# Down projections of the second block by Strassen's scheme over eight pairs of input rows, and gain sums taken as a row that is turned into columns

## The reference

```python
D_FF = 2816
def swiglu(x, w_gu, w_down):
    g, u = jnp.split(x @ w_gu, 2, axis=-1)
    return (jax.nn.silu(g) * u) @ w_down

def second_block(x, ...):
    for l in range(DEPTH):                      # DEPTH = 2
        x = layer_norm(ALPHA * x + 0.5 * swiglu(x, ffn1_w_gu[l], ffn1_w_down[l]), ln1_g[l], ln1_b[l])
        x = layer_norm(ALPHA * x + hybrid_mixer(x, ...), ln2_g[l], ln2_b[l])
        x = layer_norm(ALPHA * x + 0.5 * swiglu(x, ffn2_w_gu[l], ffn2_w_down[l]), ln3_g[l], ln3_b[l])
    return x
```

## Time and profile before

| | us |
|---|---|
| median of 3 runs | 3413.47 |
| lowest, highest | 3411.47, 3414.45 |
| the profiled execution | 3413.02 |
| its span, first to last instruction | 3411.2 |
| PE busy in the span | 3383.5 |
| DVE busy | 2519.0 |
| ACT busy | 1600.6 |
| POOL busy | 433.6 |

### The profile page before, as it was taken

How to read it: one execution, slowest core, us unless ns; L and a number is a source line. 1 busy time by engine, 2 the same in 40 slices (tenths; PEclk the granted TensorE clock), 3 DMA queues, 4 the chain that set the end, 5 groups by cost and what they waited for, 6 DMA issues and landing times.

```text
span 3411.2 us, 50605 instructions
## 1 busy us (share of the span) xinstructions
PE 3383.5 (99%) x19622; PEld 2917.4 (86%) x19622; DVE 2519.0 (74%) x3115; ACT 1600.6 (47%) x2183; POOL 433.6 (13%) x305
## 2 busy tenths in 40 slices
PE   9999999999999999999999999999999999999998
PEld 6888889988788888998899876899889988679986
DVE  8999568934999657963797388898288937978954
ACT  5555444423565444542444256544254524664433
POOL 3333010001333210001000120200020003120002
PEclk9999999999999999999999999999999999999999
DMA  3112334333221233332443221333333232123332
GB/s 127 62 62 68 108 120 161 100 117 117 69 68 62 88 127 124 131 123 98 146 147 118 93 81 56 123 117 100 119 124 112 100 123 89 60 85 138 100 123 99
DMA packets 98845, 357.23 MB, mean 105 GB/s; under 512 B 10960, under 2 KB 14544, under 8 KB 96976
## 3 DMA queue, kind: packets, MB, share of 16 engines
q1 hardware_dynamic: 85824, 305.68, 26.7%
q10 hardware_dynamic: 12816, 48.70, 3.8%
HBM read 321.83 MB, written 16.78 MB: 99 GB/s over the span
## 4 chain that ended last, share of the span: by engine, by line
PE 87%; issue 4%; DVE 3%; POOL 2%; ACT 1%; POOLq 1%; DMA 1%; DVEq 0%; SPq 0%; ACTq 0%
PE ps L2496 15%; PE ps L2498 14%; PE ps L2497 14%; PE ps L2557 10%; PE ps L2558 10%; PE ps L2556 10%; PE sc L2496 3%; PE sc L2497 3%; PE sc L2498 3%; POOLq L1452 1%; PE ps L2735 1%; DVE w_lo L1510 1%; PE sc L2810 1%; POOL DE L1454 1%; POOL Y L1447 1%
## 5 line engine op out<-in xcount | busy, mean ns | idle before, releaser
L1510 DVE TENSOR_TENSOR w_lo<-raw,w_hi 128x1024 fp32r<-128x1024 f32 x369 | 476.9, 1292 | 472.0 <-ACT w_hi L757 448.2
L757 ACT ACTIVATE w_hi<-raw 128x1024 fp32r<-128x1024 f32 x369 | 390.1, 1058 | 805.8 <-PE sc L2498 402.8
L2496 PE MATMUL ps<-h_hi,w_hi 128*128 128x512 f32 x1352 | 566.3, 419 | 10.9 <-DVE w_lo L1510 5.9
L2498 PE MATMUL ps<-h_hi,w_lo 128*128 128x512 f32 x1352 | 529.3, 391 | 0.0
L2497 PE MATMUL ps<-h_lo,w_hi 128*128 128x512 f32 x1352 | 528.5, 391 | 0.0
L870 ACT ACTIVATE w_hi<-raw 128x1024 fp32r<-128x1024 f32 x204 | 216.4, 1061 | 386.6 <-PE ps L2558 209.2
L2557 PE MATMUL ps<-h_lo,w_hi 128*128 128x256 f32 x1272 | 359.9, 283 | 0.0
L2556 PE MATMUL ps<-h_hi,w_hi 128*128 128x256 f32 x1272 | 359.7, 283 | 0.0
L2558 PE MATMUL ps<-h_hi,w_lo 128*128 128x256 f32 x1272 | 359.7, 283 | 0.0
L2496 PEld LDWEIGHTS ps<-h_hi,w_hi 128*128 128x128 f32 x1352 | 254.7, 188 | 84.7 <-issue 29.9
L2497 PE MATMUL ps<-hid_lo,w_hi 128*128 (+1 forms) x792 | 308.2, 389 | 0.0
(11 more groups left out here) (393 smaller groups left out, 7647.9 us busy)
## 6 DMA issues: line engine op xcount, KB each, us to landing
raw<-wts SPq DMA_DIRECT2D x471, 512.0 KB, 3.3
S<-wts SPq DMA_DIRECT2D x51, 512.0 KB, 3.3
A<-wts SPq DMA_DIRECT2D x51, 512.0 KB, 3.3
x<-parked ACTq DMA_DIRECT2D x7, 2048.0 KB, 8.7
h_hi<-early_hi ACTq DMA_DIRECT2D x15, 512.0 KB, 3.9
h_lo<-early_lo ACTq DMA_DIRECT2D x15, 512.0 KB, 3.5
parked<-x ACTq DMA_DIRECT2D x24, 256.0 KB, 2.0
parked<-x ACTq DMA_DIRECT2D x3, 2048.0 KB, 8.7
```

What stands on the lines that cost most here:

```text
L757: act(w_hi[:, s].rearrange("p a b -> p (a b)"), raw[:, s, :], ACT.Copy).then_inc(s_whi, 1)
L1510: tt(w_lo[:, s].rearrange("p a b -> p (a b)"), raw[:, s, :], w_hi[:, s].rearrange("p a b -> p (a b)").bitcast(F32), ALU.subtract).then_inc ...
L2496: mm(out, w_hi[:, s, b, :], hi, start=start, stop=False, skip_group_check=True)
L2498: return mm(out, w_lo[:, s, b, :], hi, start=False, stop=stop, skip_group_check=True)
```

## The change

**Down by quads.** For the four feed-forwards of the second block, `down` is replaced by `down_by_quads` on PE, with `down_quads_hi` on ACT, `down_quads_lo` on DVE and `load_down_quads` on SP. The first 6 input tiles are done as before (144 matmuls of 128x512). The other 16 are eight pairs. For six of the eight output tiles, two at a time, three quads of seven products are done over all eight pairs: 21 products of 24 matmuls of 128x256, 504 in all. The last two output tiles take 96 matmuls of 128x512.

The products need sums of the hidden layer: T2, N3 and N4, each 128x2048 (eight pairs x 256 tokens), built from hi and lo parts in ten DVE operations (`token_sum`) and then split again (ACT hi, DVE lo). One difference is put into the hidden layer itself (`token_difference`, 128x256, once for each of eight quads of gate and up). Weight blocks need four sums in each quad. DVE adds each product to x in ten half-width steps a quad (`take`), and the eight plain banks before that with `take_plain`.

**Gain rows.** `gain_sums` is replaced by `gain_rows_of`: gain and bias are the loaded operand (4 or 2 columns) and the weights the moving one (256 columns), 16 matmuls that leave a row in PSUM. ACT copies it (`gain_rows`), and `gain_columns` turns it with two matmuls of 128x2. In the norm, ACT's `h_hi` steps and DVE's `x_lo` steps stand one and two places later.

```diff
+DOWN_QUAD_FFS = (2, 3, 4, 5)
+N_DOWN_QUADS = 3
+DOWN_PLAIN = 6
+DOWN_PAIRS = (FT - DOWN_PLAIN) // 2
+DOWN_TOKEN_SUMS = 10
+DOWN_TAKES = 10
...
+        def down_w(b):
+
+            slot = (0, 2, 1)[b % 3]
+            return (w_hi[:, slot], w_lo[:, slot]) if slot < 2 else (wd_hi[:], wd_lo[:])
...
+                token_hi(TD_hi[:], TD[:], 5)
+                split_hi(pair0 + 1, 1)
+                split_hi(pair0 + 2, 0)
+                token_hi(ND_hi[:], ND[:], 7)
+                split_hi(pair0 + 2, 1)
+                eng.wait_ge(s_used, c0 + 1)
+                a11_hi(0)
+                s2_hi(0)
+                eng.wait_ge(e_used, down_tile(f, KT - 1))
+                s1_hi(0)
+                token_hi(FD_hi[:], FD[:], 9)
+                eng.drain()
+                eng.sem_inc(s_whi, 4 * N_DOWN_QUADS)
+                for q in range(N_DOWN_QUADS):
+                    b = PRODUCTS * q
+                    last = q == N_DOWN_QUADS - 1
...
+                def token_difference(q):
+                    if token_differences(f, q + 1) > token_differences(f, q):
+                        eng.wait_ge(e_ev, ev_done(f, q, TIMES1))
+                        tt(gates[:, 0, HALF:], gates[:, 0, HALF:], gates[:, 0, 0:HALF], ALU.subtract).then_inc(e_ev, 1)
 
...
+
+                for k0 in (0, 4):
+                    first_sums(0, k0)
+                for k0 in (0, 4):
+                    first_sums(1, k0)
+                split_lo(pair0 + 1, 0)
+                for k0 in (0, 4):
+                    first_sums(2, k0)
+                token_sum(ND[:], down_rows_of(hid_hi, 0, 0).bitcast(F32), TD[:], ALU.subtract, 5)
+                split_lo(pair0 + 1, 1)
+                token_lo(0, TD_lo, TD, TD_hi)
+                token_sum(ND[:], ND[:], down_rows_of(hid_lo, 0, 0).bitcast(F32), ALU.add, 6)
+                split_lo(pair0 + 2, 0)
+                eng.wait_ge(e_lo, down_token(f, 0))
+                token_sum(FD[:], down_rows_of(hid_hi, 1, 0).bitcast(F32), TD[:], ALU.subtract, 6)
+                token_lo(1, ND_lo, ND, ND_hi)
+                split_lo(pair0 + 2, 1)
+                token_sum(FD[:], FD[:], down_rows_of(hid_lo, 1, 0).bitcast(F32), ALU.add, 8)
+                s3(0)
+                s1(0)
+                block_lo(0, raw[:, 0, :])
+                eng.wait_ge(s_park, back(f))
+                take_plain(0)
+                s2(0)
+                take_plain(1)
+                block_lo(1, raw[:, 0, :])
+                for j in range(2, 5):
+                    take_plain(j)
+                block_lo(2, SD1[:])
+                for j in range(5, KT):
+                    take_plain(j)
+                token_lo(2, FD_lo, FD, FD_hi)
+                eng.drain()
+                eng.sem_inc(s_wlo, 4 * N_DOWN_QUADS)
+                for q in range(N_DOWN_QUADS):
+                    b = PRODUCTS * q
+                    last = q == N_DOWN_QUADS - 1
+
+                    if q:
+                        take_p6(q - 1)
+                        block_lo(b + 2, SD1[:])
+                        eng.wait_ge(e_ev, taken(q - 1, 9))
+                        if q == 1:
+                            eng.sem_inc(s_xp, 2)
+                        else:
+                            eng.sem_inc(s_xp, 1)
+                    block_lo(b + 3, SD3[:])
+                    take_p0(q)
...
+                        centre(0)
+
+                    take_p1(q)
+                    block_lo(b + 4, raw[:, 1, :])
...
+                c0 = pair0 * 2
+                eng.wait_ge(s_pair, FT * (f + 1) + 1)
+                eng.wait_ge(s_hidl, f * FT + DOWN_PLAIN)
+                for i in range(DOWN_PLAIN):
+                    s = i % 2
+                    eng.wait_ge(s_wlo, c0 + i + 3)
+                    for n in DOWN_ORDER:
+                        if i == 0 and n == 0:
+                            eng.wait_ge(e_act, act_done(f, quads(f) - 1, SILU0))
+                            eng.wait_ge(e_ev, ev_done(f, quads(f) - 1, TAKE_C12))
+                        if i == 0 and n == 2:
+                            eng.wait_ge(s_pair, FT * (f + 1) + 2)
+                        last = three(ps[n][:], s, n, hid_hi[:, i, :], hid_lo[:, i, :], i == 0, i == DOWN_PLAIN - 1)
+                        if i == DOWN_PLAIN - 1:
+                            last.then_inc(e_used, 1)
+                    if i < DOWN_PLAIN - 1:
+                        last.then_inc(s_used, 1)
+                eng.wait_ge(s_hidl, FT * (f + 1))
+
...
+                def product(b, bank, hi, lo, fresh):
+                    wh, wl = down_w(b)
+                    eng.wait_ge(e_lo, down_block(f, b))
+                    out = ps[bank][:, 0:HALF]
+                    for k in range(DOWN_PAIRS):
+                        mm(out, wh[:, k, :], hi[:, k, :], start=fresh and k == 0, stop=False, skip_group_check=True)
+                        mm(out, wh[:, k, :], lo[:, k, :], start=False, stop=False, skip_group_check=True)
+                        last = mm(out, wl[:, k, :], hi[:, k, :], start=False, stop=k == DOWN_PAIRS - 1, skip_group_check=True)
+                    last.then_inc(e_used, 1)
+
...
+                for q in range(N_DOWN_QUADS):
+                    b = PRODUCTS * q
+                    X, Y, Z = DOWN_BANKS[q]
+                    eng.wait_ge(e_ev, (down_taken(f, 3), down_taken(f, 6), down_take(f, 0, DOWN_TAKES - 1))[q])
+                    product(b, Y, *hid(0, 0), True)
+                    eng.wait_ge(e_lo, down_token(f, 0))
+                    product(b + 1, X, TD_hi, TD_lo, True)
+                    product(b + 2, Z, *hid(0, 1), True)
+                    eng.wait_ge(e_lo, down_token(f, 1))
+                    eng.wait_ge(e_ev, down_take(f, q, 3))
+                    product(b + 3, X, ND_hi, ND_lo, False)
+                    product(b + 4, Y, *hid(1, 0), False)
+                    eng.wait_ge(e_lo, down_token(f, 2))
+                    eng.wait_ge(e_ev, down_take(f, q, 6))
+                    product(b + 5, X, FD_hi, FD_lo, False)
...
+            def gain_rows_of(i, L, c):
+
+                eng.wait_ge(s_gl, DEPTH)
+                for k in range(KT):
+                    mm(ps[6][0:4, 0:2 * P], gb[:, L, i, k:k + 25:8], w_hi[:, :, k, :], start=(k == 0), stop=False,
+                       skip_group_check=True)
+                    last = mm(ps[6][0:2, 0:2 * P], gb[:, L, i, k:k + 9:8], w_lo[:, :, k, :], start=False,
+                              stop=(k == KT - 1), skip_group_check=True)
+                last.then_inc(s_used, 1)
+
+            def gain_columns(n):
+
+                eng.wait_ge(s_fgc, n + 1)
+                for s in range(2):
+                    last = mm(ps[6][:, 2 * P + 2 * s:2 * P + 2 * s + 2], gain_rows[:, s * P:(s + 1) * P], picks,
+                              start=(s == 0), stop=(s == 1), skip_group_check=True)
+                last.then_inc(s_fst, 1)
...
+
+                eng.wait_ge(s_wlo, c + 3)
                 bank_free()
                 for q in range(KT):
-                    gain_sums(i, L, c, 0, q, q + 1)
                     step(0, q, CENTRED[q])
                     if q == 0:
                         sums(n, order[-1])
+                eng.wait_ge(s_wlo, c + 4)
                 for q in range(KT):
-                    gain_sums(i, L, c, 1, q, q + 1)
                     step(1, q, q)
+                    if q == 1:
+                        gain_rows_of(i, L, c)
+                    elif q == 5:
+                        gain_columns(n)
 
...
+        blocks = [first[half, DOWN_ORDER[2 * q + tile]] for q in range(N_DOWN_QUADS)
+                  for half, tile in ((0, 0), (1, 0), (1, 1), (0, 1))]
+        blocks += [first[half, DOWN_ORDER[j]] for half in range(2) for j in (6, 7)]
+        return [gu.reshape(N_GU, P, CHUNK, P), rows[:DOWN_PLAIN], np.stack(blocks)]
     last = rows[DOWN_ROWS:].transpose(2, 1, 0, 3)[list(DOWN_ORDER)]
     return [gu.reshape(N_GU, P, CHUNK, P), rows[:DOWN_ROWS], last]
```

More of the change, by code:

```diff
@@ L353, in build @@
         folded_sums = small[:, 24:28]
-        low_sums = small[:, 28:32]
+        picks = small[0:4, 28:30]
+        gain_rows = place("gain_rows", [4, 2 * P], at=t_at(17))
         ps = [ctx.enter_context(nc.psum_tensor(f"ps{i}", [P, SEQ], F32)) for i in range(3)]
@@ L1274, in layer_norm @@
                 act(ps[4][:], lnt[:], ACT.Exp, scale=-0.5).then_inc(s_rstd, 1)
-                for j in range(KT + 1):
+                for j in range(KT + 2):
                     if j < KT:
@@ L2217, in layer_norm @@
+            def layer_norm(i, L, c0, order, evacuate, hv, folded_to=(), f=None):
                 n = 3 * L + i
@@ L2280, in layer_norm @@
                 eng.wait_ge(s_rstd, 6 + n)
-                for j in range(KT + 2):
+                for j in range(KT + 4):
                     if j < KT:
@@ L2649, in down, with down_by_quads, hid @@
                     last.then_inc(s_used, 1)
+            def down_by_quads(pair0, f, centre):
+                c0 = pair0 * 2
```

(22 more changed lines are left out.)

389 lines of the change are left out of this document (334 added, 55 removed).

## The result

The changed kernel takes 3430.3 us (median of five runs, 3428.9 to 3431.8), the kernel before 3413.5. The ratio is 1.005, with a 95% interval from 1.0039 to 1.0061: slower by 17 us. The forecast was 3424 in a range from 3408 to 3436, slower being the likeliest, so the time lies 6 us above it and inside the range. The profiled execution took 3430.9 us, its span 3429.1, 17.9 more than that of before.

A forecast was written before the change was run, and what follows sets the result against it. PE's matmul stream was taken to bound the kernel, with no slack for waits. From the profiled 3413.0 us: - 19.6 (down matmuls) - 7 (gain sums) + 32 (waits for DVE) + 6 (clock) = 3424 us, range 3408 to 3436.

The forecast's parts named there:

- Part 1: PE matmuls of the second block's four down projections: 4.9 us gained in each, 19.6 us in all.
- Part 3: DVE's ordered work before each down stage's first product: PE stands still 8.0 us, four times, 32 us lost.
- The cover behind it: Within a down quad, DVE's 15.9 us of work fits beside PE's 20.1 us, so no wait.
- Part 4: PE's clock halves after the gap before the first product: 6 us lost over four stages, bounds 0 and 3 each.
- Part 2: Gain sums done as rows in five norm pairs: 1.4 us gained each, 7 us in all (4.5 to 8.5).
- the turn at 0.5: The two 128x2 matmuls that turn the gain row into columns: taken at 0.5 us, between 0.24 and about 1.0.
- the rest of the norm's tail I cost at nothing: Chunk splits and `h_lo` steps behind the gain sums: same work in another order, no cost.
- PE also waits in the last quad and behind it: Rival: more waits of 1 to 2 us a stage there, 3430; chance 0.12 shared with the columns rival.
- The cover holds: Rival: DVE's work is done beside the plain down matmuls, all or mostly; 3386, up to 3406; chance 0.08.
- No drop of the clock: Rival: as forecast, but PE's clock stays up behind the down stages' gap; 3418; chance 0.14.
- Waits of about 5 to 6 us a stage: Rival: PE waits only this long in each down stage, clock or not; 3407 to 3413, no change; chance 0.08.
- The turn into columns: Rival: ACT reaches `gain_rows` late and stops PE, 1 us in each of five; 3429; chance 0.12 shared with more seams.

The follow-up runs named there:

- the version with two quads: Changed kernel with two quads instead of three, the third tile pair's wide matmuls put before the first product, and chunk splits moved earlier: 3402.4 us, ratio 0.997.
- the run with PE kept busy: Changed kernel plus 44 zero matmuls of 128x256 on PE before the last plain tile of each second-block down stage: 3424.4 us, ratio 1.0035.
- the norms alone: Changed kernel with its down projections put back as in the kernel before, keeping gain rows and the new norm order: 3407.9 us, ratio 0.9987.
- the quads alone: Changed kernel with its norms put back as in the kernel before, keeping the second block's down projections by quads: 3436.3 us, ratio 1.007.
- more work on DVE: Changed kernel with the low part of T (128x2048) computed once more on DVE before the first product: 3437.4 us, ratio 1.0073.

## Why the prediction was right, and where it was off

Step by step, by its own terms (sums over the profiled spans):

- **Part 1, -19.6 us: right.** A stage with 240 wide and 504 narrow matmuls and one of `centre_sum` would be 240 x 0.2269 + 504 x 0.1198 + 0.23 = 115.07 us. With the measured start of the product and the slow clock put on top (below) the four make about 501, and 500.8 is measured. In the version with two quads, 336 narrow matmuls and one of `centre_sum` run in 96.01 - 55.66 = 40.35 us, 0.1194 for each narrow one. By an estimate from the back-to-back formula that the prediction weighed (the Trainium skill, "TensorE: Matmul & The Clock Gate", section "Back-to-back issue gap") the narrow ones would take 36.7 us; the rows decide against it here. (The prediction's total by that formula comes to 28.6 us, not 28.3; nothing hangs on it.)
- **Part 3, +32 us: right, in sum and in its pieces.** The product starts at 40.62 to 40.85, forecast 40.7; 7.9 to 8.2 us a stage, 32.4 in all. Gaps were forecast at 1.0, 1.0, 0.1, 0.1 and 5.7, and are 1.13, 0.70, none, none and 5.39. Three experiments bear on the cause: one DVE operation more moves the product by just its 2.2 us, two less by 3.3 and no further because ACT then ends last, and taking the wait apart moves the gap to the next place.
- **The cover behind it** was costed at nothing in the quads, which holds in part by help of the slow clock: with the clock kept up, waits of 0.2 to 0.5 us appear there, one or two a stage.
- **Part 4, +6 us: right in its mechanism, short in the gross.** The slow stretch lasted 6.8 us in three stages, not 3.4. Its part behind the product's start was 3.2, 4.2, 6.0 and 5.8 us; of each, 43% is lost (a matmul every 0.21 us instead of 0.12), 8 us together. Net of the waits that it hides, 5 to 6, by the run with PE kept busy. The Trainium skill, "TensorE: Matmul & The Clock Gate", section "What's actually happening", says that the gate goes back to half rate after idling. The trace agrees: behind the four gaps of 5.4 us the granted clock is 0.50, and with the gap filled it stays at 1.00.
- **Part 2, -7 us: the term that was wrong.** Alone, the norms gave 4.6 us (0.0013 of the time, and the interval reaches from 0.0004 to 0.0022). A folded pair, from its first matmul to the row behind its 48th wide one, took 18.12 us before, 17.27 with the norms alone, in all five norms, and in the changed kernel 17.73 in the three behind a down projection and 17.27 in the other two. So the gain of a pair is 0.85 and not 1.4, just under the lower bound of 0.9, and with the quads 0.46 of it is lost again in three of five.

What went was priced right. A pair of before holds 48 wide matmuls (10.89 us at 0.2269), the sums of squares (3.03), 0.40 us that falls due behind them, and the gain matmuls with what they cost their neighbours: 18.12 - 10.89 - 3.03 - 0.40 = 3.8 us, as forecast. The 16 new ones take 1.88, forecast 1.9. The failed steps are the two terms beside them, the turn at 0.5 and "the rest of the norm's tail I cost at nothing". The 0.40 us is seen in the kernel before, PE's timeline behind the sums of squares, where the first gain matmul takes 0.43 us to the next row and the others take 0.03:

```profile
2512.07 1.02 PE L2892 MATMUL ps<-squared,ones 128*128 128x512 f32 x2
2512.53 0.57 PE L2900 MATMUL ps<-gain_and_bias,w_hi 128*128 128x4 f32 x1
2512.96 0.25 PE L2902 MATMUL ps<-gain_and_bias,w_lo 128*128 128x2 f32 x1
```

The changed kernel at the same place, and the two small matmuls (on unrounded float32 operands, two instructions each in the trace) that turn the row:

```profile
1980.32 1.12 PE L3410 MATMUL ps<-squared,ones 128*128 128x512 f32 x2 [0.43 <-POOL squared L1645]
...
1982.14 1.02 PE L3414 MATMUL ps<-squared,ones 128*128 128x512 f32 x2
1982.60 0.79 PE L2953 MATMUL ps<-h_hi,w_hi 128*128 128x512 f32 x1
1983.23 0.40 PE L2954 MATMUL ps<-h_lo,w_hi 128*128 128x512 f32 x1
...
1993.59 0.39 PE L2955 MATMUL ps<-h_hi,w_lo 128*128 128x512 f32 x1
1993.90 0.60 PE L3430 MATMUL ps<-small,gain_rows 4*128 4x2 f32 x4
1994.43 0.50 PE L2953 MATMUL ps<-h_hi,w_hi 128*128 128x512 f32 x1
1994.77 0.39 PE L2954 MATMUL ps<-h_lo,w_hi 128*128 128x512 f32 x1
```

The 0.40 us behind a matmul of unrounded operands has passed to the next one (1982.60 to 1983.23 is 0.63 instead of 0.23): whoever stands there pays it, so it is neither gained nor lost. The turn costs 0.53 us itself and makes the row before it 0.09 and the row behind it 0.11 longer, 0.73 for the 0.5 taken.

The rest is POOL. With the norms alone, PE and POOL at the sums of squares:

```profile
2505.33 1.53 POOL L1645 TENSOR_TENSOR squared<-squared,squared 128x512 f32<-128x512 f32 x1 [0.16 <-issue]
...
2505.95 1.02 PE L3409 MATMUL ps<-sq,ones 128*128 128x512 f32 x2
2506.92 1.13 PE L3411 MATMUL ps<-squared,ones 128*128 128x512 f32 x2
```

Before, POOL was done with the same square 0.19 us ahead of PE. Now the gain matmuls no longer stand in front, PE comes sooner, and its row begins 0.06 us behind POOL's end (2506.86). The sums take 3.27 us instead of 3.03 in each of the five norms, too little at a time to be listed as a wait. The turn's 0.23 and this 0.24 make most of the 0.55 us that a pair lacks. In the changed kernel the first row above shows the wait for POOL grown to 0.43 us in three norms. There the last quad ends with takes of tiles whose squares POOL has yet to add; that this is the reason is read from the order of the work and was not tested. The prediction had "PE also waits in the last quad and behind it" as a rival at 3430; of it came this 0.46 us in three norms, 1.4 us, and nothing in the quad.

The sum: 11.4 us more was forecast and 17.9 measured between the spans. The stages make 2.4 of the difference of 6.5 (the clock), the norms 3.8, and 0.3 is what is left of the start and the end. Of its signs to look for, PE's busy time fell by 12 and not by 20 us: the slow matmuls, which count as busy, explain 2 of the difference and the norms 3, the rest is not placed. The idle time grew by 29.5, forecast 30. Each stage was to last 124.4 and lasts 124.3 to 125.8.

**The rivals.** "The cover holds" fell as the prediction argued: DVE's share of 87% in the stage said nothing of its place. "No drop of the clock" fell in all four stages. "Waits of about 5 to 6 us a stage" fell by the product's start, which shows 7.9 to 8.2. The turn into columns stops PE nowhere.

## What to carry to other kernels

When a change hands work to a helper engine, count that engine's work in order up to the first point where the main engine needs it, and set it against what the main engine has to do until then; a share over the stage can be 84% and free or 87% and 8 us late. What a wait is named after is not its cause: relax it and see whether the gap goes or moves. If the backlog can't be shortened, put some of the old, wide work in front of it: one pair of tiles left as it was, with the chunk splits moved forward, turned 17 us lost into 10 gained, norms included in both. And when a small operation goes, price what takes its place from rows of its own kind, and ask which helper the main engine now meets sooner: here 0.2 us saved in front of POOL's work was waited for behind it.

## What the runs showed of the hardware

- PE's clock fell to half in all sixteen stages that have a gap of 3.5 us or more (four kernels), after three of four gaps of 2.3 us and two of four of 2.0 us, and not after the one of 1.44 us nor any of those of about 1 us. The gap near 37 us, 2.37 to 2.59 us long and in all nine traces, was followed by a slow stretch in six of them (the 2.59 of the earlier trace rows is one). In the other three, the norms alone, the quads alone and more work on DVE, no slow stretch came. So a gap of 2.0 to 2.6 us can go either way, even within one execution. The slow stretch was 3.4 or 6.8 us long after the same gap of 5.4 us, and partly ran out while PE still waited.
- 44 matmuls by zeros in a gap, in each of four stages, made a kernel 5 to 6 us faster, at the same start of the work behind them.
- Behind the 512 wide matmuls on unrounded float32 operands the next row comes 0.40 us later than in a stream, whether it has 4 columns or 512; behind the narrow ones that turn the row it is 0.11.
